# Retention state of a head pair in 64 columns instead of 128, its products in 64x64 quarters and 64-column tiles, under a new order of work

## The chip, the cores and the metric

The kernel runs on one core of one Trainium2 chip. The metric is device time in microseconds (us) of one execution, and the time of a version is the median of its runs. A core has TensorE (PE in the profile, with its weight loads shown apart as PEld), ScalarE (ACT), VectorE (DVE), GpSimd (POOL) and SyncE (SP), which here only issues DMA transfers. TensorE writes into PSUM, which has eight banks of 128 partitions x 512 floats.

## The reference, cut to what matters

Two decoder layers run over a prompt of 1024 tokens and over 8 sequences of 4 new tokens (the decode rows). Each layer is

```python
h = rmsnorm(x, norm_pre); p = h @ w_in          # 30 column blocks of 128
rq, rk, rv, rg, sq, sk, sv, sg, ca, cb, cg = jnp.split(p, idx, axis=-1)
...
y = concat([o_r, o_s, o_c]) @ w_out
return x + rmsnorm(y, norm_post)
```

with three branches: retention (6 heads of 64), stick-breaking attention (6 heads of 64) and a causal convolution. The change is about retention, which goes chunk by chunk (128 tokens) through a state S of 64 x 64 per head:

```python
def step(S, xs):
    qc, kc, vc = xs
    att = jnp.einsum('bchd,bshd->bhcs', qc, kc) * D[None]
    o = (jnp.einsum('bhcs,bshe->bche', att, vc)
         + jnp.einsum('bchd,bhde->bche', qc * q_dec[None, :, :, None], S))
    S = S * c_dec[None, :, None, None] + jnp.einsum('bchd,bche->bhde', kc * k_dec[None, :, :, None], vc)
    return S, o
```

For the decode rows the same formula runs once, as one chunk of 4 tokens, with a state per sequence and head read from `state_ret`; all final states are outputs.

## The kernel before, in words

**Layout.** Activations lie transposed: 128 features on the partitions, 1056 tokens (1024 + 32 decode rows) along the free dimension, in three column chunks of 352. All weights and activations are fp32. Each projection of a block is made of high and low parts: eight times three products of 128x352 (L1139 to L1141, `hi*hi`, `hi*lo`, `lo*hi`) per block and column chunk. There are 30 input blocks and 8 output blocks, three chunks and two layers: 228 such groups.

**Retention.** A head pair p (three per layer, six in all) shares the 128 partitions: head 0 on partitions 0 to 63, head 1 on 64 to 127. The steps of a pair are, for n = 0 to 7 (prompt chunks) and n = 8 (the decode rows):

- `dec` (POOL, L1977 on): `qd` = queries times decay, written twice, each copy with the other head's rows zeroed; `kd` = keys times decay.
- `att` (PE, L1156 on): scores of both heads in one product (L1162) and the keys turned to token-major (L1164). DVE then masks the scores (`att`), ACT copies the turned keys (`kd_tok`).
- `ro` (PE, L1166 on): for n = 1 to 7 the old state times the queries (L1176, one full-width product per head, the zeroed rows of `qd` select the head), then the scores times the values (L1180, one product of 64 output columns per head), then the state's increment (L1191, one full product for both heads). For n = 8 L1186 makes one product per decode sequence, over `state9`, 8 in all.
- `st` (DVE, L1870 and L1872): add the increment to `state`, then multiply with the decay and with a block-diagonal 0/1 matrix (`blk`), because the full product also fills the two quarters that mix the heads. The next `ro` waits for it.
- `own` (POOL, L2023), `ds9` (PE, L1198; DVE, L1880 and L1883): the increments of the 8 decode states, in two halves of four sequences, each one product over 512 columns; then `stout` (SP) writes both states, and `pair` (SP) loads the decay table and the decode states of the next pair.

`state` is [128, 128] and `state9` [128, 8, 128], with the off-diagonal quarters zero; `state9` is also a buffer for raw weights (in the first weight loads of a layer and in the output projection).

**What sets the order.** Every engine runs a list of steps that a planner writes before the program is built: `plan()` adds each step with its engine, a cost and the steps it waits for, and `Plan.order()` picks, step by step, the one that could start first, with a penalty from the table `RANKS`. On PE it also counts 0.09 us when a step starts in another tile form than the one before ended in (`tiles_of`, table `TILED`). Waits in the program are semaphores; each engine is strictly in order. The results of projections and of retention products go through a ring of three PSUM banks; scores of the stick-breaking branch have four banks of their own (`Z`), its sums one (`AV`).

A product of fp32 operands is two passes of PE in the trace: "x168" at L1176 are 84 products. The lines of the profile are those of the kernel before.

Of the kernel before, what the change touches and what calls it, by code (L numbers as in the profile page):

```python
# [10 lines left out]
ALU = mybir.AluOpType  # L11
# [55 lines left out]
def shape_constants():  # L67
# [28 lines left out]
    for p in range(PAIRS):  # L96
# [12 lines left out]
        d[p, :, D_STEP] = np.exp(P * lg[:, 0]) * HEAD_DIM  # L109
        d[p, :, D_STEP9] = np.exp(DEC_SEQ * lg[:, 0]) * HEAD_DIM  # L110
# [3 lines left out]
class Signal:  # L114
# [14 lines left out]
    def at(self, event):  # L129
# [7 lines left out]
BLOCK_ORDER = [("sq", 0), ("sk", 0), ("sv", 0), ("ca", 0), ("cb", 0), ("rq", 0), ("ca", 1), ("cb", 1), ("rk", 0), ("rv", 0),  # L137
               ("sq", 1), ("sk", 1), ("sv", 1), ("rq", 1), ("rg", 0), ("rv", 1), ("rk", 1), ("sg", 0), ("sq", 2), ("sk", 2),
               ("rk", 2), ("sv", 2), ("sg", 1), ("rq", 2), ("rg", 1), ("rv", 2), ("cg", 0), ("cg", 1), ("rg", 2), ("sg", 2)]
PROJ = BLOCK_ORDER  # L140
BLOCKS = BLOCK_ORDER + [("out", f) for f in range(KB)]
GATES = [("cb", 0), ("cb", 1), ("rg", 0), ("sg", 0), ("ln_act", 0), ("ln_act", 1), ("sg", 1), ("rg", 1), ("cg", 0), ("cg", 1), ("rg", 2), ("sg", 2)]
# [44 lines left out]
LOW_DVE = [0, 1, 3, 6, 9, 10, 12, 14, 16, 19, 23, 27, 28, 29]  # L187
# [7 lines left out]
def helper(q):  # L195
# [7 lines left out]
RANKS = {("ACT", "ln_mean"): -2.5, ("ACT", "ro"): -0.5, ("DVE", "log"): 2.5, ("PE", "ro"): -2, ("DVE", "sample_o"): 1.5, ("ACT",  # L203
         "sample_k"): 3.5, ("ACT", "weigh"): -0.5, ("PE", "all_x"): -37.5, ("PE", "sample_k"): -4.5, ("DVE", "sample_l"): -3,
         ("ACT", "pw"): 6.5, ("ACT", "root_x"): 1.5, ("SP", "glu_rest"): -6.5, ("POOL", "splo"): 2.5, ("SP", "pages"): 33,
         ("POOL", "res"): 1, ("DVE", "ln_act"): 3.5, ("PE", "ln_mean"): -41, ("SP", "oldx"): 9, ("SP", "swap"): 24.5, ("ACT",
         "gn_mean"): 1.5, ("DVE", "splo"): -1.5, ("ACT", "sample_z"): -6.5, ("POOL", "own"): 1, ("SP", "store"): 8, ("PE",
         "sample_t"): 6, ("SP", "pair"): 15, ("ACT", "ln_act"): 11.5, ("SP", "stout"): 14, ("DVE", "consts"): 24.5, ("ACT",
         "sample_t"): 3, ("ACT", "gn_var"): -1, ("ACT", "vtok"): -1, ("PE", "ln_var"): 3, ("PE", "sum_x"): -49.5, ("PE",
         "root_y"): -8, ("PE", "sample_o"): 13, ("DVE", "att"): 2, ("POOL", "rot"): 1, ("DVE", "halve"): 1, ("PE", "sample_z"):  # L210
         -94, ("ACT", "sqx"): -1.5, ("ACT", "sigmoid"): 2, ("ACT", "root_y"): 3.5, ("ACT", "k9"): 13, ("ACT", "sample_l"): 4,
         ("ACT", "hi"): -1, ("PE", "pw"): -5.5, ("PE", "proj"): 6, ("POOL", "lo"): 3, ("POOL", "dec"): -3, ("PE", "vtok"): -33,
         ("PE", "gn_mean"): -1.5, ("DVE", "ln_mean"): -1.5, ("DVE", "glu_rest"): -10, ("ACT", "wload"): 1, ("DVE", "gn_var"):
         1.5, ("SP", "vout"): 9, ("ACT", "sample_v"): 3, ("PE", "weigh"): -0.5, ("POOL", "wlo"): 1.5, ("DVE", "post"): 1, ("DVE",
         "ds9"): -1.5, ("DVE", "res"): 0.5, ("PE", "gn_var"): -3.5, ("DVE", "taps9"): 13.5, ("DVE", "ln_var"): 0.5, ("PE",
         "stop"): 2, ("POOL", "sample_z"): -4, ("ACT", "att"): -8, ("PE", "ds9"): -0.5, ("PE", "att"): -8, ("DVE", "st"): 0.5,
# [1911 lines left out]
```

## Time and profile before

| | |
|---|---|
| median of 3 runs | 1382.66 us (1379.95 to 1382.8) |
| the profiled execution, its own time | 1383.0 us |
| its span, first to last instruction | 1381.2 us |
| PE busy | 1342.9 us (97%) |
| PEld busy | 1160.4 us (84%) |
| DVE, ACT, POOL busy | 859.8, 776.5, 479.9 us |
| DMA | 116.94 MB, 85 GB/s in the mean |

Busy is the share of the span in which an engine had an instruction under way. PE's passes overlap at their ends, so what a pass costs PE is the distance from its start to the start of the next one, not its own length. In the timeline rows, passes of one line that follow each other are merged: start, time until the last one's end, line, tiles, shape and count.

### The profile page before, as it was taken

What the parts mean: (1) busy time and instruction counts of PE and PEld (TensorE: products, weight loads), DVE (VectorE), ACT (ScalarE), POOL (GpSimd) and SP (SyncE); (2) the same over time, 40 slices, a digit from 0 to 9 for tenths busy, and PEclk for the clock granted to TensorE, in tenths of its full rate; (3) what the DMA queues carried; (4) which work ended last, traced back from release to release, by engine and by line L of the source; (5) the groups of instructions that cost most, each with busy time, mean ns of one, the idle gap of its engine ahead of it and who ended that gap; (6) DMA issues with size and microseconds to landing.
All of it is one profiled execution on the core that took longest, in us unless ns stands there. A gap on an engine that the chain in (4) does not pass through costs nothing. (4 is left out here: it accounts for less than half of the span.)

```text
span 1381.2 us, 22696 instructions
## 1 busy us (share of the span) xinstructions
PE 1342.9 (97%) x8340; PEld 1160.4 (84%) x8340; DVE 859.8 (62%) x1316; ACT 776.5 (56%) x1535; POOL 479.9 (35%) x420
## 2 busy tenths in 40 slices
PE   6999999999999999999999999999999999999996
PEld 4988888887788887899988888888878888878995
DVE  3447876887632646376763687679865235554665
ACT  6565633566654665575655665256565466566542
POOL 2425342446223442031234336234551334512112
PEclk9999999999999999999999999999999999999998
DMA  7221103211042100265441111131102312016453
GB/s 248 99 54 43 51 20 113 88 50 28 25 129 81 47 31 33 80 215 180 163 128 63 51 39 58 47 121 52 44 13 93 87 48 63 16 48 203 138 175 119
DMA packets 81201, 116.94 MB, mean 85 GB/s; under 512 B 17474, under 2 KB 63042, under 8 KB 80962
## 3 DMA queue, kind: packets, MB, share of 16 engines
q1 hardware_dynamic: 65826, 59.90, 13.8%
q10 hardware_dynamic: 15264, 55.58, 12.6%
q8 instruction: 67, 1.10, 0.4%
q14 instruction: 44, 0.36, 0.1%
HBM read 89.73 MB, written 19.23 MB: 79 GB/s over the span
## 5 line engine op out<-in xcount | busy, mean ns | idle before, releaser
L1139 PE MATMUL ring<-H_hi,w_hi 128*128 128x352 f32 x1776 | 591.9, 333 | 9.5 <-DVE H_lo L984 5.9
L1141 PE MATMUL ring<-H_hi,w_lo 128*128 128x352 f32 x1776 | 572.4, 322 | 0.0
L1140 PE MATMUL ring<-H_lo,w_hi 128*128 128x352 f32 x1776 | 571.3, 322 | 0.0
L1139 PEld LDWEIGHTS ring<-H_hi,w_hi 128*128 128x128 f32 x1776 | 334.2, 188 | 44.4 <-issue 32.0
L1140 PEld LDWEIGHTS ring<-H_lo,w_hi 128*128 128x128 f32 x1776 | 335.5, 189 | 3.9
L1141 PEld LDWEIGHTS ring<-H_hi,w_lo 128*128 128x128 f32 x1776 | 334.4, 188 | 0.0
L2032 POOL TENSOR_SCALAR attend<-attend 128x512 f32<-128x512 f32 (+4 forms) x144 | 199.0, 1397 | 353.2 <-ACT attend L1459 352.9
L1843 DVE SCALAR_TENSOR_TENSOR MX<-MX,vec_sb 128x1023 f32<-128x1023 f32 (+14 forms) x120 | 163.7, 1364 | 2.1
L1699 DVE SCALAR_TENSOR_TENSOR attend<-Z,vec_sb,attend 128x512 f32<-128x512 f32 (+4 forms) x144 | 85.8, 612 | 95.0 <-ACT attend L1467 94.4
L1467 ACT ACTIVATE attend<-attend 128x512 f32<-128x512 f32 (+4 forms) x144 | 74.4, 524 | 87.3 <-POOL attend L2032 85.1
L1390 ACT ACTIVATE w_hi<-w_raw 128x1024 fp32r<-128x1024 f32 x80 | 84.4, 1055 | 54.3 <-PE ring L1141 44.2
L993 POOL TENSOR_TENSOR w_lo<-w_raw,w_hi 128x1024 fp32r<-128x1024 f32 x30 | 73.3, 2445 | 76.4 <-ACT w_hi L1390 76.2
L993 DVE TENSOR_TENSOR w_lo<-w_raw,w_hi 128x1024 fp32r<-128x1024 f32 x50 | 62.1, 1241 | 60.6 <-ACT w_hi L1390 60.5
L1459 ACT ACTIVATE attend<-Z,vec_sb 128x512 f32<-128x512 f32 (+4 forms) x144 | 75.8, 580 | 22.5 <-PE Z L1260 16.0
L1706 DVE TENSOR_TENSOR stop_lo<-attend,stop_hi 128x512 fp32r<-128x512 f32 (+4 forms) x144 | 85.7, 636 | 3.2 <-ACT stop_hi L1481 3.0
L1638 ACT ACTIVATE attend<-Z,vec_sb 128x512 f32<-128x512 f32 (+4 forms) x144 | 75.9, 578 | 16.3 <-PE Z L1270 16.2
L1987 POOL TENSOR_TENSOR qd<-ret_q,decay_sb 128x256 f32<-128x256 f32 (+1 forms) x54 | 39.8, 737 | 99.6 <-PE ring L1180 88.5
L1481 ACT ACTIVATE stop_hi<-attend 128x512 fp32r<-128x512 f32 (+4 forms) x144 | 67.9, 517 | 1.9 <-DVE attend L1699 1.8
L975 POOL TENSOR_TENSOR MX<-MX,attend 128x352 f32<-128x352 f32 x24 | 27.1, 1156 | 115.6 <-DVE MX L1972 115.6
L1254 PE MATMUL Z<-sb_q,sb_k 64*128 64x512 f32 (+5 forms) x288 | 65.6, 537 | 0.0
L1552 ACT ACTIVATE gate<-ring 128x352 f32<-128x352 f32 x54 | 25.0, 463 | 70.2 <-PE ring L1141 70.1
L1290 PE MATMUL AV<-attend 128*64 128x512 f32 (+5 forms) x288 | 62.3, 511 | 0.0
(181 smaller groups left out, 1937.5 us busy)
## 6 DMA issues: line engine op xcount, KB each, us to landing
w_raw<-in_w ACTq DMA_DIRECT2D x81, 512.0 KB, 3.6
state<-in_w ACTq DMA_DIRECT2D x25, 512.0 KB, 3.5
out_yT<-MX SPq DMA_DIRECT2D x10, 704.0 KB, 3.5
swapped<-raw_rot SPq DMA_DIRECT2D x144, 44.0 KB, 1.9
attend<-in_cache_k SPq DMA_DIRECT2D x96, 64.0 KB, 2.0
attend<-in_cache_v SPq DMA_DIRECT2D x96, 64.0 KB, 2.0
attend<-in_xT SPq DMA_DIRECT2D x3, 1408.0 KB, 13.7
attend<-out_yT SPq DMA_DIRECT2D x3, 1408.0 KB, 12.7
```

The source lines that it names most:

```text
L993: ops.tensor_tensor(wide_lo[slot(i)], raw_of(i), wide_hi[slot(i)].bitcast(F32), ALU.subtract).then_inc(sg.sem, sg.mark(i))
L1139: nc.tensor.matmul(in_ring(step), a, x, start=(n_k == 0), stop=False)
L1140: nc.tensor.matmul(in_ring(step), a, y, start=False, stop=False)
L1141: last = nc.tensor.matmul(in_ring(step), b, x, start=False, stop=(n_k == KB - 1))
L1390: nc.scalar.activation(wide_hi[slot(i)], raw_of(i), ACT.Copy).then_inc(s_whi.sem, s_whi.mark(i))
L1459: nc.scalar.activation(stop_of(u, h), Z[2 * (u % 2) + h][:, 0:n], ACT.Exp, bias=vv(p // PAIRS, V_BIAS + 2 * (p % PAIRS) + h)).then_inc(s_e ...
L1467: nc.scalar.activation(s, s, ACT.Ln, bias=1.0).then_inc(s_l.sem, s_l.mark((p, u, h)))
L1638: nc.scalar.activation(stop_of(u, h), Z[2 * (u % 2) + h][:, 0:n], ACT.Exp, bias=vv(p // PAIRS, V_BIAS + 2 * (p % PAIRS) + h)).then_inc(s_a ...
L1699: nc.vector.scalar_tensor_tensor(out=s, in0=Z[2 * (u % 2) + h][:, 0:n], scalar=vv(p // PAIRS, V_BIAS + 2 * (p % PAIRS) + h), in1=s, op0=AL ...
L1706: nc.vector.tensor_tensor(stop_lo[:, h, 0:n], stop_of(u, h), stop_hi[:, h, 0:n].bitcast(F32), ALU.subtract).then_inc(s_splo.sem, s_splo.ma ...
L1843: nc.vector.scalar_tensor_tensor(out=y, in0=glu[b][:, 0:SEQ - s], scalar=w, in1=y, op0=ALU.mult, op1=ALU.add).then_inc(s_tap.sem, s_tap.ma ...
L2032: nc.gpsimd.tensor_scalar(s, s, E_MAX, None, ALU.min).then_inc(s_min.sem, s_min.mark((p, u, h)))
```

## The change

The state of a pair is stored as [128, 64]: partitions of head h hold that head's 64 columns, and the two zero quarters are gone. Then:

- `state` times `qd` becomes two products of 64 rows x 64 columns (a quarter of the array each, on the diagonal), into the two halves of the partitions of one PSUM bank; the same for each of the 8 decode sequences (16 products in place of 8).
- The increment becomes two products of 128 rows x 64 columns, 64 wide, in place of one of 128 x 128, 128 wide.
- The two halves of `ds9` become one step: two products of 64 columns over 512, one per head. `own` is one step per head; its second half lies in the upper half of the weight buffer `raw9`, so it no longer waits for the first product.
- `st` on DVE works on 64 columns and multiplies with the decay alone (no `blk`).
- `pair` issues three DMAs in place of two, `stout` four in place of two, of half the bytes in all, in pieces of 64 floats.
- The planner gets new costs for `ro`, `ds9`, `st`, `pair`, `stout`, new `RANKS`, a table `TURNS` with a nudge for each of some 200 single steps, rules that keep steps of one kind in their order (`keep_order`), another `BLOCK_ORDER`, `GATES` and `LOW_DVE` (15 in place of 14 input blocks of a layer have their low parts made on DVE). The order of nearly all work moves.

```diff
-BLOCK_ORDER = [("sq", 0), ("sk", 0), ("sv", 0), ("ca", 0), ("cb", 0), ("rq", 0), ("ca", 1), ("cb", 1), ("rk", 0), ("rv", 0),
+BLOCK_ORDER = [("sq", 0), ("sk", 0), ("sv", 0), ("ca", 0), ("cb", 0), ("rq", 0), ("rk", 0), ("rv", 0), ("ca", 1), ("cb", 1),
...
-LOW_DVE = [0, 1, 3, 6, 9, 10, 12, 14, 16, 19, 23, 27, 28, 29]
+LOW_DVE = [0, 1, 4, 5, 6, 8, 9, 12, 14, 17, 19, 23, 25, 27, 28]
...
+TURNS = {('DVE', ('join', 5, 3)): 3, ('SP', ('store', 0, 2, 1)): -12, ('ACT', ('log', 3, 11)): 10, ('SP', ('glu_rest', 3)): -21,
...
-    if step[0] == "ro" and step[2] == QB:
-        return 2, 0
+    if step[0] == "ro":
+        return (2, 4) if step[2] == QB else (4 if step[2] else 2, 2)
...
+def keep_order(g):
+
+    last = {}
+    for node in list(g.nodes):
+        e, step = node
+        if step[0] in ("score", "log", "att", "dec", "st", "own", "rot", "swap", "vtok", "wload", "whi", "wlo"):
+            line = (e, step[0])
...
+        if line in last:
+            g.nodes[node][1].append((last[line], -5.0))
+        last[line] = node
...
-                g.add("PE", ("ro", p, n), 1.1, DVEn("att", p, n), ...
+                g.add("PE", ("ro", p, n), 2.1 if n == QB else 0.8 if n else 0.5, DVEn("att", p, n), ...
...
-        state = sb("state", [P, P])
-        state9 = sb("state9", [P, DEC_BATCH, P])
+        state = sb("state", [P, HEAD_DIM])
+        raw9 = sb("state9", [P, KB * P])
+        state9 = raw9[:, 0:512].rearrange("p (b e) -> p b e", b=DEC_BATCH)
+        v_own = [wide[:, 0:2, :].rearrange("p a n -> p (a n)")[:, 0:512], raw9[:, 512:1024]]
...
                         for h in range(2):
-                            nc.tensor.matmul(out, state[:], qd[:, n % 2, h, :], start=(h == 0), stop=False, skip_group_check=True)
+                            r = slice(64 * h, 64 * h + 64)
+                            nc.tensor.matmul(out[r, :], state[r, :], qd[r, n % 2, h, :], start=True, stop=False, skip_group_check=True)
...
-                            last = nc.tensor.matmul(out[:, q], state9[:, b, :], qd9[:, q], start=False,
-                                                    stop=(b == DEC_BATCH - 1), skip_group_check=True)
+                            for h in range(2):
+                                r = slice(64 * h, 64 * h + 64)
+                                last = nc.tensor.matmul(out[r, q], state9[r, b, :], qd9[r, q], start=False,
+                                                        stop=(b == DEC_BATCH - 1), skip_group_check=True)
...
-                        nc.tensor.matmul(increment(p, n), kd_tok[:, n % 2, :], ret_v[:, n, :], start=True, stop=True,
-                                         skip_group_check=True).then_inc(s_ds.sem, s_ds.mark((p, n)))
+                        for h in range(2):
+                            r = slice(64 * h, 64 * h + 64)
+                            last = nc.tensor.matmul(increment(p, n)[r, :], kd_tok[:, n % 2, r], ret_v[:, n, r], start=True, stop=True,
+                                                    skip_group_check=True)
...
-                    nc.tensor.matmul(bank_of(step)[:, :], kd_tok[:, QB % 2, :], v_own[:].rearrange("p b e -> p (b e)"),
-                                     start=True, stop=True).then_inc(s_ds.sem, s_ds.mark((p, QB, g)))
+                    for h in range(2):
+                        r = slice(64 * h, 64 * h + 64)
+                        last = nc.tensor.matmul(bank_of(step)[r, :], kd_tok[:, QB % 2, r], v_own[h], start=True, stop=True,
+                                                skip_group_check=True)
...
-                        nc.vector.scalar_tensor_tensor(out=state[:], in0=state[:], scalar=decay[:, D_STEP:D_STEP + 1], in1=blk,
-                                                       op0=ALU.mult, op1=ALU.mult).then_inc(
+                        nc.vector.tensor_scalar(state[:], state[:], decay[:, D_STEP:D_STEP + 1], None, ALU.mult).then_inc(
```

How the order moves, at three places. In these rows a name is the tile written, then those read; the shape is that of the output, and "waits" names the semaphores.

PE, one chunk of retention in the first pair, before:

```order
L1162 MATMUL ring<-qd,kd 128x256 [waits s_dec,s_kd]
L1164 MATMUL ring<-const,kd 128x128
L1176 MATMUL ring<-qd,state 128x128 [waits s_st,s_roc]
L1176 MATMUL ring<-qd,state 128x128
L1180 MATMUL ring<-att,attend 64x128 [waits s_attm]
L1180 MATMUL ring<-att,attend 64x128
L1191 MATMUL ring<-attend,kd_tok 128x128 [waits s_kd]
```

and one of the change (L1237, L1241 and L1256 stand for L1176, L1180 and L1191):

```order
L1222 MATMUL ring<-qd,kd 128x256 [waits s_dec,s_kd]
L1224 MATMUL ring<-const,kd 128x128
L1337 MATMUL Z<-stop_hi,negtri_r 128x320 [waits s_sphi]
L1339 MATMUL Z<-stop_lo,negtri_r 128x320 [waits s_splo]
L1337 MATMUL Z<-stop_hi,negtri_r 128x320 [waits s_sphi]
L1339 MATMUL Z<-stop_lo,negtri_r 128x320 [waits s_splo]
L1237 MATMUL ring<-qd,state 64x128 [waits s_st,s_roc]
L1237 MATMUL ring<-qd,state 64x128
L1241 MATMUL ring<-att,attend 64x128 [waits s_attm]
L1241 MATMUL ring<-att,attend 64x128
L1256 MATMUL ring<-attend,kd_tok 64x64 [waits s_kd]
L1256 MATMUL ring<-attend,kd_tok 64x64
```

The state's products are now 64 rows high on the output and the increment comes in two; here stick-breaking products stand between the scores and the rest of the chunk.

PE, the decode rows of the first pair (n = 8), before:

```order
L1340 MATMUL Z<-attend,stop 32x128 x8
L1180 MATMUL ring<-att,attend 64x32 [waits s_attm,s_st,s_roc]
L1180 MATMUL ring<-att,attend 64x32
L1186 MATMUL ring<-att,state 128x4 [waits s_state9]
L1186 MATMUL ring<-att,state 128x4 x7
L1254 MATMUL Z<-sb_q,sb_k 128x512 [waits s_copy,s_q,s_a]
```

and in the change:

```order
L1359 MATMUL AV<-attend 64x256 [waits s_a] x2
L1241 MATMUL ring<-att,attend 64x32 [waits s_attm,s_st,s_kd]
L1241 MATMUL ring<-att,attend 64x32
L1249 MATMUL ring<-att,state 64x4 [waits s_state9]
L1249 MATMUL ring<-att,state 64x4 x15
L1337 MATMUL Z<-stop_hi,negtri_r 128x128 [waits s_sphi]
```

Sixteen products stand where eight stood, and the step no longer comes right behind the products over the cached values (L1340).

DVE, the state between two chunks in the first pair, before:

```order
L1854 TENSOR_TENSOR att<-ring,const 128x256 [waits s_ro,s_att]
L1870 TENSOR_TENSOR state<-state,ring 128x128 [waits s_st,s_ds]
L1872 SCALAR_TENSOR_TENSOR state<-state,decay_sb,const 128x128 [waits s_st]
L1939 TENSOR_TENSOR MX<-MX,keep 128x256 [waits s_o,s_keepf,s_av]
L1941 TENSOR_TENSOR MX<-MX,AV 128x256 [waits s_kept]
```

and in the change:

```order
L1927 TENSOR_TENSOR att<-ring,const 128x256 [waits s_ro,s_att]
L1942 TENSOR_TENSOR state<-state,ring 128x64 [waits s_st,s_ds]
L1944 TENSOR_SCALAR state<-state,decay_sb 128x64 [waits s_st]
L1916 SCALAR_TENSOR_TENSOR MX<-MX,vec_sb 128x1012 [waits s_tap]
L2009 TENSOR_TENSOR MX<-MX,keep 128x320 [waits s_o,s_keepf,s_av]
```

The pair of state operations keeps its place behind the mask, on half the columns; another neighbour follows it.

## Rows read from the trace of the kernel before

**Rows 1.** The page: busy us of each engine, share of the span, instructions.

```profile
PE 1342.9 (97%) x8340; PEld 1160.4 (84%) x8340; DVE 859.8 (62%) x1316; ACT 776.5 (56%) x1535; POOL 479.9 (35%) x420
```

**Rows 2.** Windows of PE: us, busy (instructions), clock, DMA share, GB/s.

```profile
0.00:60.00 60.00, 48.86 (x272) 1.00 0.55 182
60.00:700.00 640.00, 634.06 (x3959) 1.00 0.26 81
700.00:1382.00 682.00, 659.95 (x4113) 0.99 0.25 79
```

**Rows 3.** Waits of PE: who waited for whom, total us, times, longest.

```profile
PE ring L1139 <- DVE H_lo L984: 5.9, 2, 4.9
...
PE ring L1176 <- DVE state L1872: 1.7, 6, 0.4
...
PE ring L1209 <- ACT attend L1533: 0.3, 1, 0.3
```

**Rows 4.** Timeline of PE, one chunk: start, us, line, tiles, rows*columns, count.

```profile
186.56 0.27 PE L1164 MATMUL ring<-const,kd 128*128 128x128 f32 x1
186.67 0.61 PE L1176 MATMUL ring<-qd,state 128*128 128x128 f32 x4
187.21 0.44 PE L1180 MATMUL ring<-att,attend 128*64 128x128 f32 x4
187.58 0.49 PE L1191 MATMUL ring<-attend,kd_tok 128*128 128x128 f32 x2
187.82 0.36 PE L1284 MATMUL Z<-stop_hi,neg_r 128*128 128x256 f32 x1
```

**Rows 5.** Timeline of PE, a chunk that comes behind 64-column products.

```profile
189.19 0.68 PE L1176 MATMUL ring<-qd,state 128*128 128x128 f32 x4
...
190.49 0.60 PE L1162 MATMUL ring<-qd,kd 128*128 128x256 f32 x2
```

**Rows 6.** Timeline of PE and of its weight loads, decode rows, first pair.

```profile
225.23 0.31 PE L1180 MATMUL ring<-att,attend 128*64 128x32 f32 x4
225.47 1.95 PE L1186 MATMUL ring<-att,state 128*128 128x4 f32 x16
227.35 1.91 PE L1254 MATMUL Z<-sb_q,sb_k 64*128 64x512 f32 x4
...
225.23 0.20 PEld L1180 LDWEIGHTS ring<-att,attend 128*64 128x64 f32 x4 [0.20 <-issue]
225.47 0.30 PEld L1186 LDWEIGHTS ring<-att,state 128*128 128x128 f32 x2
```

**Rows 7.** Timeline of PE, one half of the decode states' increment.

```profile
371.68 1.02 PE L1198 MATMUL ring<-wide,kd_tok 128*128 128x512 f32 x2
372.54 0.76 PE L1209 MATMUL ring<-MX,const 128*128 128x352 f32 x2
```

**Rows 8.** Timeline of PE, two 64-column products over 512 columns.

```profile
255.98 1.08 PE L1290 MATMUL AV<-attend 128*64 128x512 f32 x4
256.99 0.43 PE L1139 MATMUL ring<-H_hi,w_hi 128*128 128x352 f32 x1
```

**Rows 9.** Timeline of PE, a projection behind the full fp32 product of L1209.

```profile
231.41 0.60 PE L1139 MATMUL ring<-H_hi,w_hi 128*128 128x352 f32 x1
231.85 0.32 PE L1140 MATMUL ring<-H_lo,w_hi 128*128 128x352 f32 x1
232.01 0.32 PE L1141 MATMUL ring<-H_hi,w_lo 128*128 128x352 f32 x1
```

**Rows 10.** Windows of PE around the same steps of layer one and layer two.

```profile
227.50:231.00 3.50, 3.50 (x8) 0.51 0.39 96
905.00:909.00 4.00, 4.00 (x20) 1.00 0.65 193
```

**Rows 11.** Groups of DVE: line, shapes, count, busy us, mean ns, idle before.

```profile
L1872 DVE SCALAR_TENSOR_TENSOR state<-state,decay_sb,const 128x128 f32<-128x128 f32 x42 | 21.7, 518 | 1.5
L1870 DVE TENSOR_TENSOR state<-state,ring 128x128 f32<-128x128 f32 x42 | 12.1, 289 | 27.3 <-PE ring L1191 27.3
```

More of the change, by code:

```diff
@@ L200 @@
 SHARED_BY_POOL = ("wlo", "rot", "dec", "own", "lo", "splo", "res")
[L203 to L216, printed above, removed]
-         ("DVE", "lo"): -1.5, ("PE", "sample_v"): -32, ("PE", "score"): -0.5, ("DVE", "rot"): 1.5, ("DVE", "gn_mean"): -2,
-         ("DVE", "nrm"): -3, ("ACT", "log"): -1.5, ("ACT", "ln_var"): -2.5, ("ACT", "score"): 0.5, ("DVE", "q9"): 3.5, ("SP",
-         "pwload"): 22, ("SP", "hist"): 14.5, ("ACT", "proj"): 0.5, ("DVE", "taps"): 0.5}
@@ L245, in add @@
         self.nodes[node] = (cost, pairs, lag)
-        self.rank[node] = rank + RANKS.get((engine, step[0]), 0)
+        self.rank[node] = rank + RANKS.get((engine, step[0]), 0) + TURNS.get(node, 0)
         self.land[node] = land if land is not None else {"PE": 0.25, "SP": 2.25}.get(engine, 0.05)
@@ L329, in penalty @@
         return 0.02 * self.rank[n] if n[0] == "PE" else 0.25 * self.rank[n]
+def keep_order(g):
[4 more added lines that the diff above has]
+            line = (e, step[0])
+        elif step[0] == "proj":
+            line = (e, "out") if LOAD[step[1]][0] == "out" else (e, "turn") if LOAD[step[1]][0] in ("rq", "rk") and e == "ACT" else (e, step[0], step[1])
+        else:
+            continue
+        if line in last:
+            g.nodes[node][1].append((last[line], -5.0))
+        last[line] = node
 def PEn(*step): return ("PE", step)
@@ L533, in plan @@
             for k in range(2):
[L534 to L539 removed]
+                g.add("POOL", ("own", p, k), 1.1, ACTn("vtok", "rv", p, CH - 1), PEn("ds9", p - 1, 1) if p else None, rank=1)
+            g.add("PE", ("ds9", p, 1), 0.95, POOLn("own", p, 0), POOLn("own", p, 1), ACTn("att", p, QB), PEn("ro", p, QB), rank=0)
+            g.add("DVE", ("ds9", p, 1), 1.3, PEn("ds9", p, 1), rank=1)
+            g.drain[("ds9", p, 1)] = DVEn("ds9", p, 1)
+            g.add("SP", ("stout", p), 2.6, DVEn("ds9", p, 1), rank=1)
             for u, (kb, q0, width) in enumerate(UNITS):
@@ L650, in plan @@
         prev = PEn(*s)
+    keep_order(g)
     return g
@@ L716, in build @@
         qd9 = att[:, QB % 2, 0, P - NS:P]
-        v_own = wide[:, 0:2, :].rearrange("p a n -> p (a n)")[:, 0:512].rearrange("p (b e) -> p b e", b=DEC_BATCH // 2)
         keep = sb("keep", [P, 512])
@@ L893, in raw_of @@
         def raw_of(i):
-            return raw9 if in_state9(i) else w_raw[:]
+            return raw9[:] if in_state9(i) else w_raw[:]
         def signal_of(i):
@@ L1190, in _ @@
                         pe.wait_ge(s_kd.sem, s_kd.at((p, n)))
-                        nc.tensor.matmul(increment(p, n), kd_tok[:, n % 2, :], ret_v[:, n, :], start=True, stop=True,
-                                         skip_group_check=True).then_inc(s_ds.sem, s_ds.mark((p, n)))
+                        for h in range(2):
+                            r = slice(64 * h, 64 * h + 64)
+                            last = nc.tensor.matmul(increment(p, n)[r, :], kd_tok[:, n % 2, r], ret_v[:, n, r], start=True, stop=True,
+                                                    skip_group_check=True)
+                        last.then_inc(s_ds.sem, s_ds.mark((p, n)))
                 elif kind == "ds9":
@@ L1862, in _ @@
                         dve.wait_ge(s_ds.sem, s_ds.at((p, n)))
-                        nc.vector.scalar_tensor_tensor(out=state[:], in0=increment(p, n), scalar=decay[:, D_STEP:D_STEP + 1], in1=blk,
-                                                       op0=ALU.mult, op1=ALU.mult).then_inc(
+                        nc.vector.tensor_scalar(state[:], increment(p, n), decay[:, D_STEP:D_STEP + 1], None, ALU.mult).then_inc(
                             s_st.sem, s_st.mark((p, n)))
```

115 lines of the change are left out of this document (84 added, 31 removed).

## The prediction

> **What bounds the kernel now.** I read the page's busy times first: PE is under way in 97% of the span, and no other engine in over 62% [rows 1]. The windows then say where PE is not: 11.1 us of the first 60, 5.9 us of the next 640, and 22.1 us of the rest [rows 2]. The list of PE's waits has fifteen rows, from 5.9 down to 0.3 us, 26.0 us in all [rows 3]: 11.1 in the start-up, so 14.9 behind it, 5.9 of them in the middle window and 9.0 in the last. The other 13 us of the last window no wait of a product explains: they are the tail, where the final scaling and the stores follow the last product. So over some 1300 us PE works without a break, and the timeline says what each of its steps costs. The time is PE's work: a change is worth what it takes off the distance between the starts of PE's passes, and the replan can win back what is left of 14.9 us of waits.
>
> **The chunk, n = 1 to 7 (42 steps).** Before, a chunk takes 186.67 to 187.82 = 1.15 us [rows 4]: four full passes over the state in 0.54, four passes in 64-column tiles in 0.37, two full passes of the increment with 0.24 to the next start. A full pass of 128 columns costs 0.11 (186.56 to 186.67), so 0.54 is 3 x 0.11 and one of 0.21: 0.10 is paid where the tile form changes. In L1180 the two heads' passes run side by side, in two column tiles: four passes of 128 columns would be 0.44 one after the other, and they take 0.37 with a form change in it.
>
> After, the state's pair is two tiles, 128 columns, two passes, then a form change: the same shape of work as L1180, 0.37. Below this it can hardly go; from above it is four passes in turn, 0.54. I take 0.37, since L1180 is the nearest row. The scores times values then stay in their form with the increment, so 0.37 less the change, 0.27. The increment's pair is 64 columns wide, between L1180 at 128 (0.37) and at 32 columns (225.23 to 225.47 = 0.24 [rows 6]): 0.28, less some 0.05 for a first weight load that now hides behind the pass before it, 0.23. That is 0.87, and 0.10 more where the step ahead ends in the whole array: 0.97. Where a chunk came behind tiled products it took 189.19 to 190.49 = 1.30 before [rows 5], and would take 0.87. By the order 8 of the 42 chunks stand so before, 13 in the change: 34 x 1.15 + 8 x 1.30 = 49.5 us before, 29 x 0.97 + 13 x 0.87 = 39.4 after. **-10.1 us**; from above, with 0.54, -3.0. For n = 0 (6 steps) L1180 and L1191 take 0.61 (187.21 to 187.82), and 0.27 + 0.23 after: **-0.7**.
>
> **The decode rows, n = 8 (6 steps).** 225.23 to 227.35 = 2.12 before [rows 6], of which L1186 is 1.88: sixteen passes of four columns at 0.12, though each has hardly a column to stream. They cost what a full pass costs, so it is the weight load of 128 columns that sets them. After, sixteen pairs of passes with 64-column loads. In the same rows four 64-column loads in two tiles are over in 0.20, two 128-column loads take 0.30, so loads of two tiles go side by side. From below: 16 x 0.055 (half of 0.11, a load of half the columns) and a form change, 1.0; from above, loads in turn, 1.88 as before. I take 1.1, nearer to the loads that the rows show, so 1.35 with L1180: **-4.6 us**, 0 at the upper end.
>
> **The decode states' increment (6 pairs of steps become 6 steps).** 371.68 to 372.54 = 0.86 each, 1.72 for two [rows 7]. Two 64-column products over 512 columns take 255.98 to 256.99 = 1.01 with the exit [rows 8], 1.11 with the entry: **-3.7 us**.
>
> **The order.** A projection behind a full fp32 product pays 231.41 to 231.85 = 0.44 for its first pass in place of 0.16 [rows 9]; the order has 38 such places, 32 before: **+1.7**. The other switches of form are as many as before, or ten fewer; nothing for them.
>
> **Waits.** The six waits for the state, 1.7 us [rows 3], end with L1870 and L1872, 289 + 518 ns [rows 11]. Both now run on half the columns and L1872 loses its second full operand; half of 807 ns is gone, as much as the longest of these waits (0.4): **-1.7**. In the opposite direction, the scores' mask on DVE used to hide behind the state's passes: 0.54 of cover are now 0.37. By the order only one chunk (pair 4, n = 7) has its scores right ahead of it with nothing between, and six of 72 stick-breaking units have less PE work between their scores (L1254) and their sums (L1268) than any had before; some tenths each: **+2.5**. The other waits I leave at what they are: a plan of the same kind, with more nudges, can do better or worse.
>
> **Costed at nothing.** `own` without its wait: POOL is busy 35% [rows 1]. DVE has some 17 us less in L1870 and L1872, half of 33.8 [rows 11], and one more low part per layer: it is busy 62%. Each of six pairs issues three DMA instructions more on SP: the states are written many projections before the next pair's first `dec`, and the last pair's before the output projection needs `raw9`. If that cover were gone at each pair, a wait like the longest that PE has, 4.9 us [rows 3], would come six times, 29 us; no place in the order is near it.
>
> **The clock.** After the decode rows of layer one the granted clock is 0.51 for 3.5 us, so 1.2 GHz; in the same steps of layer two it stays at 2.4 GHz [rows 10]. What ran ahead of it were 48 passes in 32-column tiles and the sixteen four-column passes. The fall is worth up to 1.7 us, and the change pulls those two apart; I count half, **-0.8**.
>
> **Sum.** -10.1 - 0.7 - 4.6 - 3.7 + 1.7 - 1.7 + 2.5 - 0.8 = -17.4. The profiled execution took 1383.0, its span and 1.8 us around it, which gives 1365.6; the median of the runs, 1382.66, lies 0.3 lower. I predict **1365.5 us**.
>
> **A rule against it.** The two state products of a chunk lie in different rows of the array and write the same PSUM bank, each half of its partitions. No row here has that: the two row tiles of L1254 write two banks (Z), and the two column tiles of L1180, which share a bank, share all rows. If such passes can't run side by side, the state's pair takes 0.54, 42 x 0.17 = 7.1 us, and the decode rows stay at 2.12, 4.6 us: 11.7 in all, **1377**. The Trainium skill, "TensorEngine Tiling (Array Packing)", section "Gotcha 1: PSUM Pressure", says just this: different row tiles cannot access the same PSUM bank at once. By that rule the time is 1377. I give it a small chance, since L1180 shows two halves of one bank written at once and here too the halves differ.
>
> **The rivals.** (a) Forecast, 1365.5: **0.57**. Its own range is 1360 to 1371, from 1.0 to 1.5 for the decode rows and some 3 us of waits either way. (b) The replan also takes out half of the 13.2 us of waits that remain past the start beside the state's, and adds none: 1365.5 - 2.5 - 6.6 = **1356.4**: **0.18**. For it speaks that these are few places, ten rows; against, that each wait is short and its cause another, so that moving a step for one moves others. (c) Passes in turn in one bank, 1377: **0.12**. (d) Slower, by the clock: the change makes 32 quarter passes of four columns in each of six places, and 48 small ones stay in six others. If PE falls to 1.2 GHz behind all twelve, as behind one of them in layer one, that is 12 x 1.7 = 20.4 on top of the sum without its -0.8: **1386.7**. It ends over the old time only from about eleven falls on; against it speaks layer two, where the clock held. **0.06**. The Trainium skill, "TensorE: Matmul & The Clock Gate", "Part 1: The HAM clock gate", has activity release a throttle that is the default; layer one agrees in kind, layer two shows that these steps need not trip it. (e) New waits of over 15 us, a retention or stick-breaking chain that is late at each of its places, some 0.3 us at 50 of them: 1382 and above, **0.07**. That PE isn't the bound I exclude by its 97%.
>
> **How the numbers follow.** A measurement of this kernel can tell about 0.2%, 2.8 us, from no change: faster is below 1380, slower above 1385. (a), (b) and nearly all of (c) are faster, 0.85; a tenth of (c) and half of (e) are same, with parts of (d), 0.07; slower is what is left of (d) and (e), 0.08. For 8 in 10 the range takes in (a), nearly all of (b) and of (c): 1354 to 1379.
>
> **What would show it.** Right: the state's four passes in 0.37, starting in pairs a few ns apart, in one bank; 0.87 to 0.97 per chunk; 1.35 for the decode rows; one increment of 1.0; PE busy some 17 us less at the same 97%. Wrong: four starts 0.11 apart, L1249 still near 1.9, a clock below 1 behind L1249, or rows in PE's list of waits over 1 us that were not there.

## The result, and the profile after

The changed kernel takes **1347.03 us** (median; 1346.48 to 1348.08) where the kernel before took 1382.72 beside it: ratio 0.975, 95% interval 0.9735 to 0.9765. It is faster by 35.7 us. The forecast was -17.4, and the time lies 7 us under the low end of the range.

The page of the changed kernel, busy us of each engine, and the windows of PE (columns as in [rows 2]; the last one ends with the span):

```profile
PE 1317.3 (98%) x8532; PEld 1136.4 (84%) x8532; DVE 834.3 (62%) x1306; ACT 772.9 (57%) x1535; POOL 464.9 (35%) x418
```

```profile
0.00:60.00 60.00, 48.34 (x272) 1.00 0.54 177
60.00:700.00 640.00, 636.03 (x4145) 1.00 0.26 78
700.00:1346.00 646.00, 632.94 (x4119) 0.99 0.26 82
```

The span fell by 35.2 us (1381.2 to 1346.0). PE's busy time gives 25.6 of it [rows 1], its idle time the other 9.6: 38.3 us before, 28.7 after. By windows [rows 2] the idle time went from 11.1 to 11.7 in the start-up, from 5.9 to 4.0 in the middle, and from 21.3 (to 1381.2, the end of the span) to 13.1 in the last. PE is still the bound.

Where the busy time went, the timeline of PE shows: one chunk behind 64-column products (it answers to [rows 5]), and the decode rows of the first pair (to [rows 6]).

```profile
188.25 0.49 PE L1359 MATMUL AV<-attend 128*64 128x384 f32 x2
188.67 0.44 PE L1237 MATMUL ring<-qd,state 64*64 64x128 f32 x4
189.04 0.44 PE L1241 MATMUL ring<-att,attend 128*64 128x128 f32 x4
189.31 0.28 PE L1256 MATMUL ring<-attend,kd_tok 128*64 128x64 f32 x4
189.52 0.49 PE L1323 MATMUL Z<-sb_q,sb_k 64*128 64x128 f32 x4
...
200.66 0.26 PE L1241 MATMUL ring<-att,attend 128*64 128x32 f32 x4
200.85 1.10 PE L1249 MATMUL ring<-att,state 64*64 64x4 f32 x32
201.88 0.33 PE L1337 MATMUL Z<-stop_hi,negtri_r 128*128 128x128 f32 x1
```

The state's four quarter passes take 188.67 to 189.04 = 0.37, the scores times values 0.27, the increment 0.21: a chunk of 0.85 where it was 1.30. The decode rows take 200.66 to 201.88 = 1.22, before 2.12. The list of PE's waits, first and last rows:

```profile
PE ring L1199 <- DVE H_lo L1040: 4.9, 1, 4.9
PE Z L1426 <- ACT raw_rot L1488: 4.5, 1, 4.5
PE ring L1222 <- POOL kd L2061: 1.5, 2, 1.1
...
PE Z L1353 <- ACT attend L1709: 0.3, 1, 0.3
PE AV L1359 <- ACT attend L1650: 0.3, 1, 0.3
```

Thirteen rows, 17.9 us, in place of fifteen and 26.0 [rows 3]. The six waits for the state are gone, and so are most of those of the weights and of the stick-breaking sums.

For the comparisons below PE's time is also added up by steps, each from its first start to the first start of the next step, so that a step carries a wait in front of the next step and whatever the next step's first pass pays (`weigh`, L1353 on, and `stop`, L1337 on, belong to the stick-breaking branch). The columns are the kernel before, the changed one and the experiments; us, from each profiled execution.

| steps | before | after | e1 | e2 | e6 | e7 | e8 | e5 | e9 | e10 |
|---|---|---|---|---|---|---|---|---|---|---|
| `ro`, n = 1 to 7 (42) | 52.2 | 35.9 | 35.7 | 52.7 | 52.7 | 52.2 | 43.5 | 35.9 | 35.9 | 35.7 |
| `ro`, n = 0 (6) | 4.2 | 2.7 | 2.7 | 4.0 | 4.0 | 4.2 | 4.2 | 2.7 | 2.7 | 2.7 |
| `ro`, n = 8 (6) | 12.3 | 7.4 | 7.5 | 12.2 | 7.4 | 7.5 | 12.3 | 13.0 | 11.7 | 13.1 |
| `ds9` | 11.4 | 6.7 | 6.0 | 10.3 | 10.8 | 10.6 | 11.5 | 6.6 | 6.6 | 6.0 |
| `att` | 28.1 | 31.2 | 31.6 | 29.5 | 29.5 | 28.1 | 30.4 | 31.0 | 31.0 | 31.6 |
| `weigh` | 105.9 | 104.6 | 105.1 | 109.3 | 108.2 | 105.8 | 105.8 | 105.5 | 105.7 | 106.3 |
| `stop` | 62.9 | 58.0 | 61.0 | 57.9 | 58.0 | 62.8 | 62.9 | 57.9 | 58.0 | 60.9 |
| projections | 907.5 | 903.3 | 907.2 | 909.6 | 904.3 | 906.3 | 907.0 | 909.1 | 905.8 | 911.7 |
| all PE steps | 1364.0 | 1330.5 | 1338.1 | 1364.7 | 1353.5 | 1354.4 | 1355.6 | 1340.5 | 1337.5 | 1348.5 |

### The profile page after: what moved, and what is told of

Same layout as the page of the kernel before. It is cut to its first block, busy times and chain, and to the rows that moved or that the text cites. A ratio compares the mean times of both kernels' runs of the same rounds, so it can differ in the third digit from the quotient of the medians.

```text
span 1346.0 us, 23077 instructions
## 1 busy us (share of the span) xinstructions
PE 1317.3 (98%) x8532; PEld 1136.4 (84%) x8532; DVE 834.3 (62%) x1306; ACT 772.9 (57%) x1535; POOL 464.9 (35%) x418
## 4 chain that ended last, share of the span: by engine, by line
PE 94%; ACT 2%; DVE 1%; POOL 1%; issue 1%; DMA 0%; SPq 0%; ACTq 0%; DVEq 0%; POOLq 0%
PE ring L1199 23%; PE ring L1201 21%; PE ring L1200 21%; PE Z L1323 4%; PE AV L1359 4%; PE Z L1337 2%; PE Z L1339 2%; PE ring L1278 2%; PE ring L1222 2%; PE Z L1353 2%; PE Z L1354 1%; PE ring L1241 1%; PE ring L1301 1%; PE ring L1237 1%; PE ring L1290 1%
## 5 line engine op out<-in xcount | busy, mean ns | idle before, releaser
L2101 POOL TENSOR_SCALAR attend<-attend 128x512 f32<-128x512 f32 (+4 forms) x144 | 188.9, 1328 | 319.4 <-ACT attend L1528 319.3
L1916 DVE SCALAR_TENSOR_TENSOR MX<-MX,vec_sb 128x1023 f32<-128x1023 f32 (+14 forms) x120 | 166.7, 1389 | 2.2
L1049 DVE TENSOR_TENSOR w_lo<-w_raw,w_hi 128x1024 fp32r<-128x1024 f32 x52 | 66.8, 1285 | 66.0 <-ACT w_hi L1459 65.9
L1049 POOL TENSOR_TENSOR w_lo<-w_raw,w_hi 128x1024 fp32r<-128x1024 f32 x28 | 67.7, 2418 | 82.3 <-ACT w_hi L1459 82.3
L1777 DVE TENSOR_TENSOR stop_lo<-attend,stop_hi 128x512 fp32r<-128x512 f32 (+4 forms) x144 | 82.0, 609 | 10.5 <-ACT stop_hi L1550 10.2
L2009 DVE TENSOR_TENSOR MX<-MX,keep 128x384 f32<-128x384 f32 (+5 forms) x60 | 42.3, 704 | 38.6 <-PE AV L1359 33.8
## 6 DMA issues: line engine op xcount, KB each, us to landing
attend<-in_xT SPq DMA_DIRECT2D x3, 1408.0 KB, 10.8
attend<-out_yT SPq DMA_DIRECT2D x3, 1408.0 KB, 11.1
```

Of the source, the lines that this page charges most:

```text
L1049: ops.tensor_tensor(wide_lo[slot(i)], raw_of(i), wide_hi[slot(i)].bitcast(F32), ALU.subtract).then_inc(sg.sem, sg.mark(i))
L1777: nc.vector.tensor_tensor(stop_lo[:, h, 0:n], stop_of(u, h), stop_hi[:, h, 0:n].bitcast(F32), ALU.subtract).then_inc(s_splo.sem, s_splo.ma ...
L1916: nc.vector.scalar_tensor_tensor(out=y, in0=glu[b][:, 0:SEQ - s], scalar=w, in1=y, op0=ALU.mult, op1=ALU.add).then_inc(s_tap.sem, s_tap.ma ...
L2101: nc.gpsimd.tensor_scalar(s, s, E_MAX, None, ALU.min).then_inc(s_min.sem, s_min.mark((p, u, h)))
```

## The experiments

Each experiment is set against the kernel before, run beside it (medians of 1379.56 to 1381.18 us where 1382.72 stood beside the changed kernel), so across experiments it is the ratios that compare.

**Products or order: e1 and e2.** The first question is what each half of the change is worth alone. e1 has the narrow state, its products, its DMAs and its DVE steps, in the order of the kernel before (planner untouched, `ds9` once per pair, at the place of its second half):

```
 def orders():
-    return plan().order()
+    o = plan().order()
+    return {e: [s for s in o[e] if not (s[0] == "ds9" and s[2] == 0)] for e in o}
```

> The 64-column state and its products, with every step in the order of the kernel before (the first half of ds9 falls out, nothing else moves). Theory A (two separate gains: the products' own saving of some 22 to 24 us, and some 11 to 13 us of PE waits that only the new order takes out): 1358 to 1362, waits of PE past the first 60 us still 11 to 15 us. Theory B (the waits went because the retention steps and the DVE operations between them are shorter, whatever the order): 1346 to 1351, waits past the start below 7 us. Both expect 0.85 us a chunk, 1.2 us the decode rows.

Measured: 1355.9 us (1355.11 to 1357.05) where the kernel before took 1379.56, ratio 0.9823, interval 0.9806 to 0.9839. That is some 24 us from the products alone. The time lies 2 us under theory A's range and 5 over theory B's. What the two say of the waits decides for A: PE's listed waits past the first 60 us are 13.1 us in e1, and 6.2 in the changed kernel.

e2 is the reverse: the changed kernel's planner, tables and nudges, with the 128-wide state and its products. `own` and `ds9` stay in two halves, the first at the changed kernel's place, the second a little later:

```
-    return plan().order()
+    g = plan()
+    o = g.order()
...
+        put("POOL", ("own", p, 1), t + 2.0, {})
...
+        put("PE", last, t + 5.0, {("ds9", q, 0): at("PE", ("ds9", q, 1)) for q in range(DEPTH * PAIRS)})
```

> The 128-column state and products of the kernel before in the order of the changed one; the second half of ds9 and of own is put some us behind the first, since they share a buffer. Theory A: 1383 less 11 to 13, so 1370 to 1374 (up to 3 more if the moved half comes late), PE waits past the start near 6 us. Theory B: 1380 or more, since nothing is shorter.

Measured: 1379.55 us, ratio 0.9997, interval 0.9986 to 1.0007. So the new order, as e2 builds it, is worth nothing with wide products, and 9 to 10 us with narrow ones (1355.9 to 1347.03; 0.9823 to 0.975). The two don't add up, and neither theory says why. The windows of e2 give a part of the answer. First the three that answer to [rows 2], then three pairs: from the start of the decode rows of pairs 1, 3 and 4, and the 3.4 us behind.

```profile
0.00:60.00 60.00, 48.50 (x278) 0.94 0.55 182
60.00:700.00 640.00, 633.94 (x3947) 0.99 0.25 78
700.00:1380.20 680.20, 665.69 (x4119) 0.99 0.26 83
```

```profile
375.54:377.70 2.16, 2.16 (x23) 1.00 0.03 8
377.70:381.10 3.40, 3.40 (x13) 0.50 0.47 149
883.08:886.30 3.22, 3.22 (x33) 1.00 0.23 65
886.30:889.70 3.40, 3.40 (x11) 0.50 0.45 131
1087.48:1091.10 3.62, 3.62 (x26) 1.00 0.21 55
1091.10:1094.50 3.40, 3.40 (x9) 0.50 0.05 13
```

The order does give back idle time here too, 38.3 to 32.1 us. But PE's busy time rises by 5.2 (1342.9 to 1348.1), because the granted clock falls to half, 1.2 GHz, five times behind the start-up: four times right behind the wide decode rows (pairs 1, 3, 4, 5), once at 394.8 behind a wait of 2.5 us. The kernel before has one such fall [rows 10]; the changed kernel's profiled execution has none until its tail. (The profiled execution of e2 took 1382.07 us, among the slowest of ten; the others need not have all five.) What one costs the timeline of e2 tells, in the projection behind pair 1:

```profile
375.72 1.95 PE L1260 MATMUL ring<-att,state 128*128 128x4 f32 x16
377.53 0.48 PE L1213 MATMUL ring<-H_hi,w_hi 128*128 128x352 f32 x1
...
378.10 0.50 PE L1215 MATMUL ring<-H_hi,w_lo 128*128 128x352 f32 x1
378.39 0.50 PE L1213 MATMUL ring<-H_hi,w_hi 128*128 128x352 f32 x1
378.68 0.50 PE L1214 MATMUL ring<-H_lo,w_hi 128*128 128x352 f32 x1
```

The products start 0.29 apart in place of 0.16 [rows 9]: 3.4 us hold 11.7 of them and not 21, so a fall costs 1.5 to 1.6 us, and five 8. That is close to the order's gain with narrow products. This became **theory C**: rows of some 2 us (1.8 of them four-column passes) let the clock fall behind them, the narrow ones of 1.2 us (1.0) don't, and the falls ate the order's gain in e2. How far the last part holds, e6 and e7 show together below.

**How much hangs on the planner's tables: e3 and e4.** e3 is the changed kernel with `TURNS` empty; e4 has the narrow products and the new costs with the old `BLOCK_ORDER`, `GATES`, `LOW_DVE` and `RANKS`, no `TURNS` and no `keep_order`.

```
-TURNS = {('DVE', ('join', 5, 3)): 3, ('SP', ('store', 0, 2, 1)): -12,
...
+TURNS = {}
```

> The changed kernel with the table TURNS emptied; all other tables, costs and keep_order stay and the planner orders anew. If the nudges of single steps carry the order's part of the gain: 1354 to 1360, with waits of PE back at 12 us or more. If the other tables carry it: within 3 us of 1347.

> The changed kernel's products and step costs, planned with the old BLOCK_ORDER, GATES, LOW_DVE and RANKS, without TURNS and keep_order. Theory A: like the old order, 1357 to 1364. Theory B: 1346 to 1352, since any order would do.

Measured: e3 1466.37 us, ratio 1.0624 (1.0607 to 1.0642); e4 1466.94 us, ratio 1.0621 (1.0602 to 1.064). Both expectations missed by over 100 us. PE's longest waits in e3, then in e4:

```profile
PE Z L1280 <- DVE MX L1991: 25.8, 2, 15.5
PE Z L1310 <- ACT attend L1666: 10.3, 11, 3.0
```

```profile
PE Z L1313 <- ACT attend L1669: 24.9, 23, 4.0
PE Z L1299 <- DVE stop_lo L1737: 12.4, 18, 1.7
```

PE sits idle for 109 us in e3 and 96 in e4 (span less busy), and the mean clock is 0.964 and 0.961. So these tables can't be taken out one by one: without them the planner makes another plan. The useful splits are those that keep one finished order and change the products, as e1 and e2 do.

**The decode rows and the clock: e5 and e6.** e5 is the changed kernel with the rows issued twice; e6 is e2 with the decode rows alone as quarters of the wide states.

```
-                        for b in range(DEC_BATCH):
+                        for b in [*range(DEC_BATCH), *range(DEC_BATCH)]:
```

```
-                            last = nc.tensor.matmul(out[:, q], state9[:, b, :], qd9[:, q], start=False,
+                            for h in range(2):
+                                r = slice(64 * h, 64 * h + 64)
+                                last = nc.tensor.matmul(out[r, q], state9[r, b, r], qd9[r, q], start=False,
```

> The changed kernel with the decode rows' 32 quarter passes (L1249) issued twice in each of the six places n = 8, so that these rows take about as long as the wide ones did (the decode outputs hold the state's part twice; nothing else is changed). The pairs of passes start 59 ns apart, so 16 more pairs are 0.95 us, 5.7 us in six places. Theory C (a stretch of some 2 us of four-column passes, with thin steps behind it, is what lets the granted clock fall, and it was this that ate the new order's gain when the products were wide): four to six falls to half clock behind n = 8, each worth some 1.6 us, so 1359 to 1363 us, the granted clock near 0.99. Theory D (the falls belong to the wide passes or to chance, not to the length of the stretch): 1353 us, no fall, the clock 0.997 as in the changed kernel.

> The wide products in the new order (as in e2, which came out even with the kernel before), with one part narrowed: the decode rows as 16 pairs of 64x64 quarters of the same 128-wide states. Theory C (five falls of the clock right behind wide decode rows took some 8 us in e2): the rows themselves -5 us (2.05 to about 1.2, six times), and the falls at 377.7, 886.3, 1091.1 and 1227.6 us go, another -6 to -8 us: ratio to the kernel before 0.990 to 0.992, granted clock 0.995 or more. Theory D (the new order as such is worth nothing with wide products, the falls are not tied to these rows): -5 us alone, ratio 0.996, the clock still 0.988.

e5: 1354.68 us (1352.44 to 1358.11), ratio 0.980, interval 0.9782 to 0.9819. Its windows, from the start of the decode rows of pairs 1, 3, 4 and 5, and the 3.4 us behind:

```profile
368.69:371.20 2.51, 2.51 (x72) 1.00 0.02 7
371.20:374.60 3.40, 3.40 (x14) 0.50 0.47 154
865.87:869.60 3.73, 3.73 (x83) 0.99 0.27 75
869.60:873.00 3.40, 3.40 (x13) 0.50 0.44 126
1067.33:1070.90 3.57, 3.57 (x75) 1.00 0.23 61
1070.90:1074.40 3.50, 3.50 (x10) 0.51 0.07 18
1201.16:1204.10 2.94, 2.94 (x76) 0.99 0.00 0
1204.10:1207.50 3.40, 3.40 (x14) 0.50 0.02 5
```

Four falls, behind the same four pairs as in e2. The rows took 5.6 us more and the projections 5.8; the profiled span is 10.0 longer than the changed kernel's. The median of the runs lies only 7.7 higher, below theory C's 1359 and near theory D's 1353, so the time alone doesn't tell them apart. The falls do: D expected none. C holds in where and whether. Its time was set too high by some 4 us against the median; the profiled execution, with its four falls, is the slowest of the five (1358.11, clock 0.989), and the others, at 0.991 to 0.993, were not looked at window by window.

e6: 1370.55 us (1368.92 to 1371.73), ratio 0.9917, interval 0.9899 to 0.9935, within theory C's 0.990 to 0.992; D's 0.996 is outside. The four falls behind decode rows are gone, the one behind the wait stays (391.4 us), the rows fell from 12.2 to 7.4 and the projections from 909.6 to 904.3. The mean clock, 0.993 in the profiled execution, stayed under the 0.995 expected. Narrowing six places of 2 us took off 9 to 11 us, half of it in steps that were not touched.

**Two terms by themselves: e7 and e8.** Both are the kernel before, in its own order and with its wide states: e7 with the edit of e6, e8 with the state's products of the chunks as quarters.

```
-                            nc.tensor.matmul(out, state[:], qd[:, n % 2, h, :], start=(h == 0), stop=False, skip_group_check=True)
+                            r = slice(64 * h, 64 * h + 64)
+                            nc.tensor.matmul(out[r, :], state[r, r], qd[r, n % 2, h, :], start=True, stop=False, skip_group_check=True)
```

> The kernel before, in its own order, with the decode rows alone as pairs of 64x64 quarters of the 128-wide states. It measures one term of the forecast (-4.6 us) by itself. The forecast: -4.6 us, ratio 0.9967. The step ledger of the changed kernel (n = 8 from 2.05 to 1.23 us, six times): -4.9, and by theory C also the one fall at 227.6 us goes, -1.6: -6.5 us, ratio 0.9953. If the two quarters of a pair had to go in turn because they write one PSUM bank: 0, ratio 1.000.

> The kernel before, in its own order, with the state's two products of each of 42 chunks alone as 64x64 quarters of the 128-wide state (the increment stays a full product). The forecast's term for this: 0.54 to 0.37 us, 42 times, -7.1 us, ratio 0.9949. By the step ledger (a chunk fell by 0.39 us, of which the increment explains some 0.14): -0.25 us each, -10.5 us, ratio 0.9924. If the row tiles went in turn in their one bank: 0, ratio 1.000.

e7: 1373.47 us where the kernel before took 1380.7, ratio 0.994, interval 0.9922 to 0.9957. The rows gave 4.8 us, the fall of [rows 10] did not come, and 0.9953 is within the interval; the forecast's 0.9967 is not. e8: 1372.97 us, ratio 0.9938, interval 0.9921 to 0.9956: both -7.1 and -10.5 lie in it, 0 does not. A chunk in e8:

```profile
185.09 0.27 PE L1164 MATMUL ring<-const,kd 128*128 128x128 f32 x1
185.29 0.44 PE L1177 MATMUL ring<-qd,state 64*64 64x128 f32 x4
185.66 0.44 PE L1181 MATMUL ring<-att,attend 128*64 128x128 f32 x4
186.03 0.49 PE L1192 MATMUL ring<-attend,kd_tok 128*128 128x128 f32 x2
186.27 0.37 PE L1285 MATMUL Z<-stop_hi,neg_r 128*128 128x256 f32 x1
```

The state's pair takes 0.37 where it took 0.54 [rows 4], as forecast, and the entry from the full array now falls before it: 185.09 to 185.29 = 0.20, where 0.11 stood. By the steps that is -8.7 in `ro` and +2.3 in `att`, so -6.4.

**Old and new order once more: e6 beside e7.** Both have wide products but for the decode rows, and no fall behind these rows in either; they differ in the order. e6 takes 1370.55 us, e7 1373.47: the new order gives 2.9 us here (the two intervals overlap), not the 9 to 10 that it gives with narrow products. So the falls behind the rows are not the whole answer to e2. Another part is made by e2's and e6's own edit, as the rows of e6 show:

```profile
389.58 0.68 DVE L1960 TENSOR_TENSOR state<-state,ring 128x512 f32<-128x512 f32 x1
390.30 0.75 DVE L1963 SCALAR_TENSOR_TENSOR state<-state,decay_sb,const 128x512 f32<-128x512 f32 x1
390.96 0.51 DVE L1968 TENSOR_TENSOR MX<-MX,ring 128x352 f32<-128x352 f32 x1
391.53 0.66 PE L1213 MATMUL ring<-H_hi,w_hi 128*128 128x352 f32 x1 [2.53 <-DVE MX L1968]
```

The second half of `ds9`, which the edit puts here, takes a bank of the ring and keeps DVE busy right ahead of the operation that PE waits for (the first two rows). PE stands for 2.5 us, and the fall at 391.4 comes behind this wait. The changed kernel doesn't have this half; there PE goes on at 383.29 us without a wait, before the same operation has run (383.94). Wait and fall are some 4 us; e2 has both too, from 391.1 on. That leaves some 2 to 3 us of the difference between wide and narrow products unexplained, little more than such runs can tell.

**Which passes run side by side: e9.** The trace doesn't say which head a quarter pass belongs to. e9 is the changed kernel with the same 32 passes in another order:

```
-                        for b in range(DEC_BATCH):
-                            q = slice(b * DEC_SEQ, (b + 1) * DEC_SEQ)
-                            for h in range(2):
+                        for h in range(2):
+                            for b in range(DEC_BATCH):
+                                q = slice(b * DEC_SEQ, (b + 1) * DEC_SEQ)
```

> The changed kernel with the decode rows' 32 quarter passes (L1249) in another order: all sixteen of the first head, then all sixteen of the second, in place of a head after the other in each batch row. Work, data and results are the same. Theory S (the pairs of starts 7 ns apart are the two heads' quarters, which run side by side although both write one PSUM bank, and this is what makes the rows cheap): passes of one head can't pair, 32 of them at 50 to 60 ns, the six places from 7.4 to about 12 us, and by theory C the falls of the clock come back with rows of 2 us: 1356 to 1359 us, clock near 0.99. Theory U (a pair is the two passes of one fp32 product, or each quarter pass costs some 29 ns by itself, whatever stands beside it): no change, 1347 us.

Measured: 1354.02 us (1351.27 to 1357.7), ratio 0.9807, interval 0.9789 to 0.9826: 7 to 8 us slower than the changed kernel, for the same work. The timeline of PE in e9, decode rows of the first pair:

```profile
199.40 0.26 PE L1241 MATMUL ring<-att,attend 128*64 128x32 f32 x4
199.59 1.82 PE L1249 MATMUL ring<-att,state 64*64 64x4 f32 x32
...
201.33 0.33 PE L1337 MATMUL Z<-stop_hi,negtri_r 128*128 128x128 f32 x1
```

The 32 passes take 199.59 to 201.33 = 1.74 where they took 1.03. One by one their starts stand 58 to 59 ns apart within a head, and only the last passes of the first head and the first of the second lie between each other (6 to 52 ns). In the changed kernel they come in pairs, 7 and 52 ns apart by turns. So a pair is two heads, and passes of one row tile start no closer than 58 ns: theory S. With the rows at 1.9 us the clock falls again, behind pairs 3, 4 and 5 (0.50 from 866.8, 1068.2 and 1201.3 us on, 3.4 us each). The time is 2 us under S's range; U's 1347 is excluded.

**The same rows in the old order: e10** is e1 with the edit of e5.

> The narrow products in the old order (as in e1, 1355.9 us beside 1379.6 before) with the decode rows' quarter passes issued twice (the decode outputs hold the state's part twice). Products: +5.6 us. Theory C2 (whether rows of 2 us trip the clock is set by what stands around them: the old order has one such place, behind pair 0, the new one four): one fall, +1.6, so some 7 us over e1, ratio to the kernel before 0.987 to 0.988. Theory C1 (any such rows trip it at most places, in either order): three to five falls, 10 to 14 us over e1, ratio 0.990 to 0.992.

Measured: 1367.46 us (1362.82 to 1368.04), ratio 0.9896, interval 0.9878 to 0.9913. Over e1 that is 0.73%, 10 us: 5.6 for the rows and three falls, behind pairs 1, 4 and 5 (from 360.0, 1029.0 and 1203.1 us on), at 1.6. The number lies between the two expectations and its interval reaches into both; the three falls speak for C1. Pair 0, behind which the kernel before has its one fall, shows none here.

## Why the prediction was wrong

The direction and the mechanism of the products were right, the size was half. By profiled spans e1 is 26.0 us shorter than the kernel before, where the forecast had -21.6 for the products, the state's waits and the clock; the changed kernel is another 9.2 shorter than e1, where the forecast had +4.2 for the order and new waits.

- **The step that failed is the one on the waits**: "The other waits I leave at what they are", with +2.5 for new ones and +1.7 for the order. I took PE's waits as a property of the program that a replan leaves alone on average. Measured, the new order is worth 9 to 10 us with the narrow products (e1 against the changed kernel, intervals that don't touch). From e1's trace to the changed kernel's, the span falls by 9.2 us, and PE's idle time gives 7.4 of it (36.1 to 28.7), the end 1.6 of these (from the last product to the end of the span 11.69 us in e1, 10.10 in the changed kernel, 11.75 before); by steps `stop` falls by 3.0 and the projections by 3.9, gaps included. The list of PE's waits behind the start-up bounds what a replan can win there: of its 14.9 us the products alone leave 13.1, the new order 6.2. So the order took nearly half of the bound, and the tail, which I had left as it was, came on top. My rival (b) had this mechanism, at 1356.4, and I gave it 0.18; the time lies 9 us below it too. That "a plan of the same kind can do better or worse" stood in the forecast; a price for "better" did not. The +1.7 itself came: 38 projections begin with a first pass of 0.4 us or more, 32 before; it is in the 9.2.
- **Chunks, n = 1 to 7**: -10.1 forecast. Measured -16.3 in `ro` and +3.1 in `att`, where the entry of 0.10 into the tiles now falls: -13.2. After the change the sum of mine holds: 39.4 forecast, 35.9 + 3.1 measured. Before it I had 49.5, and the steps took 52.2: only 18 of the 42 took 1.15, the other 24 took 1.23 to 1.43, where I had counted 8 at 1.30. The state's pair at 0.37 and the increment at 0.21 (0.23 forecast) came as worked out.
- **n = 0, n = 8, `ds9`**: -0.7, -4.6, -3.7 forecast; -1.5, -4.9, -4.7 measured. With the chunks and the 1.7 us of waits for the state, which stand in the steps ahead of `ro`, that is -20.8 forecast and -26.0 measured.
- **The state's waits** went as forecast, though DVE's two steps shrank by far less than the half that I took:

```profile
L1944 DVE TENSOR_SCALAR state<-state,decay_sb 128x64 f32<-128x64 f32 x42 | 17.1, 407 | 1.5
L1942 DVE TENSOR_TENSOR state<-state,ring 128x64 f32<-128x64 f32 x42 | 9.2, 219 | 27.8 <-PE ring L1256 27.8
```

  626 ns in place of 807 [rows 11]: half the columns (and, in L1872, one operand less) took off a fifth of L1872 and a quarter of L1870. The waits are gone in e1 too, so the new order wasn't needed. In e8, where only the state's products are narrow and DVE still takes 807 ns, they stay; in e2, with wide products in the new order, one is left:

```profile
PE ring L1177 <- DVE state L1873: 1.6, 6, 0.4
PE ring L1250 <- DVE state L1950: 0.2, 1, 0.2
```

  So either would have done: the shorter steps that hand the state on (the increment on PE and the two on DVE, not told apart here), or the order.
- **The clock**: -0.8 forecast, one fall of 1.5 to 1.6 us gone. Rival (d) had the sign the wrong way round: the change doesn't bring falls, it takes away the long rows behind which they come. e5, e9 and e10, with rows of 2 us again, show three or four falls each; e2 shows what the new order would have met with wide decode rows. I had the one fall in [rows 10] before me and did not ask which other places were near it.
- **Rival (c)**, passes in turn in one bank, is excluded: 0.37 per pair, and e9 shows what turns would cost (1.74 for the rows in place of 1.03). The rule of the Trainium skill, "TensorEngine Tiling (Array Packing)", section "Gotcha 1: PSUM Pressure", that different row tiles cannot access one PSUM bank simultaneously, doesn't hold for this form, two row tiles that write different partitions of one bank; that they may write the same partitions was not tried.

What stays open: why rows of 2 us trip the clock at some pairs and not at others. In e2, e5, e9 and e10 pair 2 shows no fall behind its rows; pair 0 shows one only in the old order with wide rows (the kernel before, e8), which in turn shows none behind the other five. Some 2 to 3 us of what the new order gives with narrow products and not with wide ones are open too. And the 9 us of the order can't be put down to single nudges: e3 and e4 show only that taking them all away costs far more than 9.

## What to carry to other kernels

Where PE is busy 97% of the time, still price the waits that a replan can remove: their list bounds the gain, and here nearly half of it came. Test a change of products and a change of order each with the other held fixed; if the two don't add up, look at the granted clock, and at the waits that the test's own edit brings. Issue passes for different row tiles alternately, since passes of one tile went in turn here (58 ns each, in place of 59 for two). Look at the clock behind long stretches of four-column passes: here the steps behind 1.7 us of them could pay 1.5 us more, those behind 1.0 us of them, where PE didn't wait, paid nothing.

## What the runs showed of the hardware that I had not expected

- Two 64x64 quarter passes on the diagonal, writing the two halves of one bank, start 7 ns apart, and a pair of four-column passes costs 59 ns; alone, each costs 58 to 59 ns (e9). So the second head is free if its pass comes next, and costs full price if it comes sixteen passes later.
- Behind 1.7 to 1.9 us of four-column passes the granted clock was 0.50 for 3.4 us at three or four of six places, whether these passes are full (e2) or quarters (e5, e9, e10), and at one of six in the kernel before and e8; behind 1.0 us of them it stayed at 1.00 (changed kernel, e1, e6, e7); in e4, where PE also waited 0.9 us ahead of them, it fell at 376.3. PE was busy all the while (3.40 of 3.40 us). The Trainium skill, "TensorE: Matmul & The Clock Gate", "Part 1: The HAM clock gate", has the throttle as the default that activity releases; these runs agree in that the clock came back each time with PE at work.
- The cost of the falls lies in other steps than their cause: from e2 to e6 the rows gave 4.8 us and the projections 5.3.
